# Reordering the masks, the lower product and the spread in a chunked delta rule

## The reference

```python
g = jnp.cumsum(chunks(g), axis=-1)
decay = jnp.exp(jnp.where(tri_incl, g[..., :, None] - g[..., None, :], -jnp.inf))
k_beta = k * beta[..., None]
lower = jnp.where(tri_strict, jnp.einsum('nbhid,nbhjd->nbhij', k_beta, k) * decay, 0.0)
rhs = jnp.concatenate([v * beta[..., None], k_beta * jnp.exp(g)[..., None]], -1)
sol = lax.linalg.triangular_solve(lower + jnp.eye(CHUNK, dtype=f32), rhs,
                                  left_side=True, lower=True, unit_diagonal=True)
u, w = sol[..., :DV], sol[..., DV:]
attn = jnp.where(tri_incl, jnp.einsum('nbhid,nbhjd->nbhij', q, k) * decay, 0.0)
...
def step(state, xs):
    v_new = u_c - jnp.einsum('bhck,bhkv->bhcv', w_c, state)
    o = jnp.einsum('bhck,bhkv->bhcv', q_c, state) + jnp.einsum('bhij,bhjv->bhiv', attn_c, v_new)
    state = state * jnp.exp(gl)[..., None, None] + jnp.einsum('bhck,bhcv->bhkv', k_c, v_new)
```

## Time and profile before

| | us |
|---|---|
| Median of 3 runs | 3335.11 |
| Lowest and highest run | 3326.7, 3336.2 |
| Profiled execution, its own time | 3328.85 |
| Span of the profiled execution, first to last instruction | 3327.4 |
| TensorE busy in the span | 3072.8 |
| VectorE, ScalarE, GpSimd busy in the span | 1593.7, 1075.9, 1077.9 |

### The profile page before, as it was taken

One profiled execution on the slowest core, in us unless ns is written; L12 is line 12 of the kernel. 1 busy time (PEld: TensorE's weight loads), 2 busy tenths in 40 slices (PEclk: granted clock), 3 DMA queues, 4 the chain that ended last, 5 costly groups with the idle time before them and its releaser, 6 DMA issues. The chain is left out here.

```text
span 3327.4 us, 44247 instructions
## 1 busy us (share of the span) xinstructions
PE 3072.8 (92%) x15074; PEld 2540.9 (76%) x15074; DVE 1593.7 (48%) x2713; ACT 1075.9 (32%) x2399; POOL 1077.9 (32%) x1209
## 2 busy tenths in 40 slices
PE   6999997959998899989979999899998999999898
PEld 5888885648786788878768888788887788887686
DVE  3554004535664555556585455865555433233433
ACT  2211004334544555542243333433333211111321
POOL 2222241066665766410073333543331000000122
PEclk9999998979998999999989999999999999999999
DMA  3212115422324211125723222232223333233443
GB/s 136 88 75 77 76 57 168 156 76 67 82 72 107 59 52 53 67 77 178 239 69 122 91 76 83 69 117 93 77 79 110 132 98 101 91 95 117 154 123 99
DMA packets 284414, 329.18 MB, mean 99 GB/s; under 512 B 33281, under 2 KB 224641, under 8 KB 279937
## 3 DMA queue, kind: packets, MB, share of 16 engines
q1 hardware_dynamic: 238632, 265.84, 25.1%
q0 software_dynamic: 12384, 45.09, 3.8%
q10 hardware_dynamic: 33280, 16.78, 1.8%
HBM read 210.73 MB, written 116.92 MB: 98 GB/s over the span
## 5 line engine op out<-in xcount | busy, mean ns | idle before, releaser
L2074 PE MATMUL ff_bank<-ff_x_hi,ff_w_lo 128*128 128x512 f32 x1240 | 487.6, 393 | 31.7 <-DVE ff_w_lo L2254 22.2
L2075 PE MATMUL ff_bank<-ff_x_lo,ff_w_hi 128*128 128x512 f32 x1240 | 486.5, 392 | 0.0
L2076 PE MATMUL ff_bank<-ff_x_hi,ff_w_hi 128*128 128x512 f32 x1240 | 486.3, 392 | 0.0
L2057 POOL TENSOR_TENSOR ff_w_sum<-ff_w_raw 128x512 f32<-128x512 f32 x210 | 301.2, 1444 | 492.4 <-DVE ff_w_lo L2254 434.0
L296 PE MATMUL in_h_ps<-in_x_hi,in_w_lo 128*128 128x512 f32 x704 | 277.5, 394 | 25.7 <-POOL in_w_lo L252 25.7
L2074 PEld LDWEIGHTS ff_bank<-ff_x_hi,ff_w_lo 128*128 128x128 f32 x1240 | 235.4, 190 | 84.0 <-DVE ff_w_lo L2254 25.0
L2464 PE MATMUL fd_acc<-fd_w_hi,fd_a_lo 128*128 128x512 f32 x704 | 279.2, 397 | 11.5 <-DVE fd_a_lo L2448 11.5
L2466 PE MATMUL fd_acc<-fd_w_hi,fd_a_hi 128*128 128x512 f32 x704 | 280.4, 398 | 0.0
L2465 PE MATMUL fd_acc<-fd_w_lo,fd_a_hi 128*128 128x512 f32 x704 | 278.4, 395 | 0.0
L297 PE MATMUL in_h_ps<-in_x_lo,in_w_hi 128*128 128x512 f32 x704 | 276.8, 393 | 0.0
L298 PE MATMUL in_h_ps<-in_x_hi,in_w_hi 128*128 128x512 f32 x704 | 276.4, 393 | 0.0
(11 more groups left out here) (381 smaller groups left out, 6558.5 us busy)
## 6 DMA issues: line engine op xcount, KB each, us to landing
ff_w_raw<-w_gate_up SPq DMA_DIRECT2D x44, 1024.0 KB, 5.2
scratch_hT<-in_out SPq DMA_DIRECT2D x22, 1024.0 KB, 3.9
fd_a_raw<-scratch_hid SPq DMA_DIRECT2D x176, 128.0 KB, 2.1
dr_qkv<-scratch_hT SPq DMA_DIRECT2D x16, 768.0 KB, 5.1
in_w_raw<-w_in POOLq DMA_DIRECT2D x22, 512.0 KB, 3.9
scratch_hid<-ff_first SPq DMA_DIRECT2D x44, 256.0 KB, 2.3
scratch_hid<-ff_second SPq DMA_DIRECT2D x44, 256.0 KB, 2.3
fd_w_raw<-w_down SPq DMA_DIRECT2D x22, 512.0 KB, 5.0
```

The source lines that it names most:

```text
L2057: pool.tensor_tensor(w_sum[:, SUM_SLOT[m]], w_raw[:, b, one], w_raw[:, b, two], op).then_inc(w_sum_done, 1)
L2074: pe.matmul(acc, w_lo[:, wm, ws], x_hi[:, xm, k], start=first_mm, stop=False, skip_group_check=skip)
L2075: pe.matmul(acc, w_hi[:, wm, ws], x_lo[:, xm, k], start=False, stop=False, skip_group_check=skip)
L2076: return pe.matmul(acc, w_hi[:, wm, ws], x_hi[:, xm, k], start=False, stop=last_mm, skip_group_check=skip)
```

## The change

GpSimd makes the mask below the diagonal first, then the other, and both of them before the decayed q. The factor of L's rows is no longer multiplied in by GpSimd; VectorE takes it as the scalar of an instruction that multiplies twice, one for each head. The k by k product gets a semaphore of its own, on which L waits. VectorE spreads the inverses ahead of attention's product.

```diff
-        gram_done = s.sem("gram_done")
+        gram_k_done, gram_done = s.sem("gram_k_done"), s.sem("gram_done")
...
-                    sp.wait_ge(masked, 3 * TILES)
+                    sp.wait_ge(masked, 2 * TILES)
...
             def masks(m):
                 pool.wait_ge(dec_done, m + 1)
+                reached(pool, L_done, m)
+                pool.tensor_tensor(dec[:, 0], dif[:, m % 2], each(below[:]), ALU.mult).then_inc(masked, 1)
                 reached(pool, attn_done, m)
                 pool.tensor_tensor(dec[:, 1], dif[:, m % 2], each(upto[:]), ALU.mult).then_inc(masked, 1)
-                reached(pool, L_done, m)
-                pool.tensor_tensor(dec[:, 0], dif[:, m % 2], each(below[:]), ALU.mult).then_inc(masked, 1)
-                pool.wait_ge(masked, 3 * m + 2)
-                pool.wait_ge(made_done, 3 * (m + 1))
-                pool.tensor_tensor(dec[:, 0], dec[:, 0], heads(made[:, m % 2, 2]), ALU.mult).then_inc(masked, 1)
...
                 if m is not None:
+                    masks(m)
                     decayed(m)
-                    masks(m)
...
                 for h in range(HEADS):
-                    pe.matmul(b0[:, h], qkv[:, m % 3, HEADS + h], qkv[:, m % 3, HEADS + h], start=True, stop=True)
+                    last = pe.matmul(b0[:, h], qkv[:, m % 3, HEADS + h], qkv[:, m % 3, HEADS + h], start=True, stop=True)
+                last.then_inc(gram_k_done, 1)
...
-                reached(act, masked, 3 * (m - 1))
+                reached(act, masked, 2 * (m - 1))
...
-                reached(dve, masked, 3 * (m - 1))
...
             def p_lower(m):
-                dve.wait_ge(gram_done, m + 1)
-                dve.wait_ge(masked, 3 * m + 3)
+                dve.wait_ge(gram_k_done, m + 1)
+                dve.wait_ge(masked, 2 * m + 1)
...
-                dve.tensor_tensor(L[:, m % 3], b0[:], dec[:, 0], ALU.mult).then_inc(L_done, 1)
+                for h in range(HEADS):
+                    op = dve.scalar_tensor_tensor(L[:, m % 3, h], b0[:, h], made[:, m % 2, 2, h:h + 1], dec[:, 0, h],
+                                                  ALU.mult, ALU.mult)
+                op.then_inc(L_done, 1)
 
             def p_attention(m):
                 dve.wait_ge(gram_done, m + 1)
+                dve.wait_ge(masked, 2 * m + 2)
...
                 if first:
                     p_lower(m)
-                    p_attention(m)
                 if base:
                     spread(e)
+                if first:
+                    p_attention(m)
```

## The result

The changed kernel takes 3301.11 us in the median of four executions (3300.12 to 3303.30). Four of the kernel before, the three that the prediction had and one more, have a median of 3330.90. The ratio is 0.9922, with a 95% interval of 0.9901 to 0.9942: 26 us less, between 19 and 33 (the two medians alone are 30 apart). The forecast was 3316, in 3306 to 3330. Two sizes are involved: the base of 3335.1 was the median of three executions and stood 4 to 9 us above what more executions gave (3326.2 to 3330.9 in five sets of 4 to 35), and the gain itself was under-sized. The profiled executions leave the base out: 3328.85 before and 3301.84 after (span 3300.4) are 27.0 apart, where 18.7 were forecast. So 8.3 us are to be explained.

What follows compares the result with a forecast made beforehand. The substitution loop was taken to bound most delta-rule rounds, just above TensorE's own order. Terms of 1.9, 1.7, 13.9 and 1.2 made 18.7 us off 3335.1, giving 3316 us, in 3306 to 3330.

Steps and rivals of the forecast that it cites:

- Masks: L, behind GpSimd's `below` alone, starts 1.35 after the substitution instead of 4.86, 3.5 us less; decays ready with 0.4 to spare.
- L on VectorE: Four instructions that multiply twice take 1.12 us against 0.69 for L, adding 0.43 to the substitution loop.
- Own signal: L's gate from TensorE comes 2.7 us earlier, serving the five rounds that waited for k by q.
- substitution loop: Delta-rule round from one store of the inverses through L, its store, blocks' load and substitution to the next: 20.75 us.
- TensorE's order: TensorE's own work in a delta-rule round, from L1151 to the end of L1180: 19.68 us.
- The queue, the 19.9 loop: L's early store lands 1.05 behind the inverses on the DMA queue, so the changed substitution loop takes 19.9 us, not 17.65.
- Attention's product and the norm: Attention's product, now behind the spread on VectorE, delays the norm and so L1096: counted as 0.1 us a round.
- Term (3): The 13 delta-rule rounds give back 17.8 us of waits for U less 3.9 for loop and attention's product: 13.9 us.
- Term (4): At the last spread, L of tile 15 ends 2.2 us earlier, 1.0 of it counted in term (3): 1.2 us gained.
- Queue keeps the loop: Rival: L's store takes its whole 2.0 behind the inverses, loop 20.85; 7.5 us gained, 3328; chance 0.26.
- No queueing: Rival: L's store lands in 2.0 wherever issued, loop 17.65, TensorE binds; 27 us gained, 3308; chance 0.15.
- Slower: Rival: inverses land late and hold up VectorE's order; 10 us lost if landing takes 9.4, 3345; chance 0.07.

Runs made afterwards that it cites:

- masks_only: The changed kernel with L waiting for k by q and attention's product ahead of the spread, as before the change: 3325.05 us, ratio 0.9975 to the kernel before.
- undo_signal: The changed kernel without k by k's own signal, so L waits for k by q again: 3324.41 us, ratio 0.9993 to the kernel before.
- load_last: The changed kernel with a later tile's q, k, v load issued behind L's store and its blocks' load: 3295.21 us, ratio 0.9907 to the kernel before.
- spread6: The changed kernel with its spread written six times, to make TensorE wait for U: 3364.19 us, ratio 1.0100 to the kernel before.
- load_last_tail: load_last with five loads for the next stage issued behind the load of the last inverses: 3298.58 us, ratio 0.9905 to the kernel before.
- the filled kernels: The kernel before with extra identity products ahead of TensorE's wait for U: eight took 3328.11 us, four took 3333.19 us.
- no_masks: The kernel before with k by k's own signal and the spread's new place, GpSimd's masks and factor unchanged: 3324.69 us, ratio 0.9987.
- spread_only: The kernel before with only the spread moved ahead of attention's product: 3326.38 us, ratio 1.0000.
- before_filled4: The kernel before with four extra identity products ahead of TensorE's wait for U: 3333.19 us, ratio 1.0012.
- spread6_filled: spread6 with eight identity products on TensorE ahead of its wait for U: 3354.03 us, ratio 1.0069 to the kernel before.

## Why the prediction fell short, point by point

**Masks.** As forecast: `below` is GpSimd's first operation behind a substitution, L never waits for it in the 13 rounds, and L starts 3.08 after the inverses' store in place of 4.86. The cover of 0.4 us for the decays was not there: the substitution ends 12.8 us after L1149 and the decays 13.4, where I had 13.4 and 13.0, and `below` waits for ScalarE in 10 rounds. It costs nothing, since k by k ends later still, as the forecast had said.

**L on VectorE.** 1.13 us against 0.69, as priced (+0.43), and the undisturbed 21.08 of `masks_only` against 20.65 fits it.

**Own signal.** Forecast as serving the five rounds that k by q held up. It serves all of them: without it the change is worth 2 us (`undo_signal`), and with it alone some 5. I had the substitution loop (20.75) and TensorE's order (19.68) and took the k by q waits for the slow clock's doing. By `masks_only` the chain through k by q and VectorE, 20.65 a round, ran beside them the whole time. The sum was not hurt, since the change opens both; a forecast of the parts would have been.

**The queue, the 19.9 loop.** Its rule was tested in the first rounds alone. There L's store is issued while the big load and the inverses' load are under way:

```profile
702.09 0.38 SPq L977 DMA_DIRECT2D dr_u_blk<-scratch_blocks_U  x1
703.07 0.44 SPq L980 DMA_DIRECT2D scratch_blocks_L<-dr_L  x1
706.85 1.38 SPq L987 DMA_DIRECT2D dr_blk<-scratch_blocks_L  x4
```

The store takes 3.8 us and the blocks' load goes out 3.78 behind its issue, some 0.5 behind the landing of the inverses. I had taken 1.05 behind it, between 0.8 and 2.0, so the sign was right and the price too high, the lower bound included. That a store is told of only behind the earlier transfers is the order which the Trainium skill states ("DMA: Bandwidth & Descriptors", section Queues, rings and completion order). The trace agrees: 3.8 us instead of 2.0, without the full 2.0 that I had added for the strictest case. In the steady rounds it doesn't arise: k by k, not the mask, lets L go, its store is issued 4.24 after the inverses' and lands in 2.0. The loop of 19.9 doesn't bind there.

**Attention's product and the norm.** I counted 0.1 a round for it. The waits show 0.3 to 0.5 us at L1093 in 6 of the rounds (such a round takes 19.9 to 20.2 instead of 19.47), and `load_last` shows their cause: the inverses land 4.2 after their issue, the spread is late, and the norm behind it. Over the 12 rounds that is 0.31 a round. So my deduction of 3.9 us and the measured 3.7 agree in size by luck: what takes them is the inverses' load, not L's store.

**Term (3), the step that failed.** It reads "if nothing but TensorE bound them they would give back all 17.8", less 3.9. Per round that is 21.57 - 13.9 / 13 = 20.50; measured are 19.78, 0.72 less, 8.6 us over 12 rounds. What was wrong with it is that it removed the waits and kept all the rest of the round as it stood. Without the waits for U (16.85 us in these 12 rounds) TensorE took 242.0 us before and takes 237.3 after, against its own 12 x 19.47 = 233.6. Nearly all of the 8.6 is the difference between those 242.0 and 233.6; the 3.7 above them is what I had deducted anyway. Two things had been inside the 242.0. One is the slow clock. I wrote "slow clock included" in what would show the forecast, and so held it to be a property of the stage. It stood in three stretches, 13.6 us in sum, each right behind a wait of 1.77 to 1.96 us at L1151; one of them:

```profile
819.55 0.44 PE L1151 MATMUL dr_b<-dr_ident,dr_U 128*128 128x128 f32 x2 [1.96 <-DVE dr_U L1449]
824.18 1.97 PE L1096 MATMUL dr_b<-dr_ident,dr_qkv 128*128 128x128 f32 x8
```

The eight transposes in the second row take 1.09 us at full clock, a round later. What the stretches cost can be read in this trace: without the wait that ends it, each of the nine rounds at full clock takes 19.68 or 19.69, and the three with a stretch take 21.15, 22.57 (23.53 - 0.96) and 21.16. That is 1.47 + 2.89 + 1.48 = 5.8 us, 0.43 for each us at 1.2 GHz. That these stretches went because the waits went is not shown by an experiment in this kernel: `spread6` shows that such waits can cost the clock, and neither of the two traces of the change has a stretch at 1.2 GHz between 740 and 988 us. The other thing is TensorE's round itself: I read 19.68 off one round, and every full-clock round of this trace has it, but 19.47 is what a round needs that holds no wait for U, 0.21 x 12 = 2.5 us. The three add up: 233.6 + 5.8 + 2.5 = 241.9. So term (3) took TensorE's time between the waits for fixed, and 8.4 us of it were not.

**Term (4).** -0.1 in place of 1.2. L of the last tile ends 1.2 earlier against the reader of its round, as forecast, but the queue takes it back. L's store takes 2.50 where it took 2.04 (983.97 to 986.47 against 1011.99 to 1014.03; no run says why), and the load of the last inverses goes out later:

```profile
999.68 0.33 SPq L968 DMA_DIRECT2D scratch_blocks_U<-dr_inv  x1
1002.99 0.37 SPq L977 DMA_DIRECT2D dr_u_blk<-scratch_blocks_U  x1
```

```profile
1005.64 0.44 PE L1149 MATMUL dr_b<-dr_ident,dr_U 128*128 128x128 f32 x2 [2.00 <-DVE dr_U L1450]
```

From the store to the load are 3.31 us; the kernel before has 2.41 at this place and both have 1.5 in an ordinary round. In `load_last_tail`, where attention's first five loads are issued behind it, it is 1.50: it is those loads on the queue that delay the store. TensorE waits 2.00 for this U, against 1.75 before.

**Rivals.** "Queue keeps the loop" is out: no wait for U is left in 13 rounds. "No queueing" named 27 us and 3308, and 27.0 is what the profiled executions show, but not for its reason: the store of L does queue where it is early, and the waits of 17.8 were given back together with 4.7 of TensorE's own time (8.4 less the 3.7 of the late norm). It had a chance of 0.15, and its number came right by luck. "Slower" did not occur; the inverses' landing is 4.2 in the median and 4.9 at most.

**Still open.** What brings a stretch at 1.2 GHz is not settled by the length of a wait: in the kernel before 1.77 to 1.96 us did and 2.43 (at 906.73) did not, the filled kernels and `no_masks` have a stretch behind 1.45, and `spread_only` none behind 2.94. Nor is it settled what the 5.8 us were worth in time while both chains stood. `before_filled4` takes 4.1 us less over the 12 rounds with a whole clock, and `spread_only`, which has one too, 3.1 less (pace 21.31); these are single executions of kernels with another order, and neither is faster as a whole. So some 3 to 4 us is an estimate, and the rest of the 5.8 came only with the two chains.

## What to carry to other kernels

Write down every chain that closes on itself in a round, the short waits that look harmless included, and compare their lengths: here 20.65, 20.75 and 19.47. Where two are within 0.1 us, freeing one is worth little and freeing both is worth their whole distance to the third, so a part that measured little alone may carry most of the gain: the signal gave 5 us, hardly clear of nothing, and its removal takes all but 2. Find the bound's own time for a round in the round with no idle and full clock, not in a typical one, and ask of each wait of 1.5 to 2 us on TensorE whether a stretch at 1.2 GHz stands behind it. On a DMA queue put a small load that someone waits for ahead of a big one that is needed a round later: moving one issue took the pace from 19.78 to 19.47, and the times suggest some 5 us more (the intervals overlap).

## What was not expected of the hardware

- 2.34 us of idle ahead of each U in an otherwise busy round brought ten stretches at 1.2 GHz in twelve rounds, 3.4 to 10.2 us each, and cost 1.5 us a round; eight products of the identity in the idle time took them away (`spread6`, `spread6_filled`). A stretch was seen behind 1.45 us of idle, and none behind another 2.94. Each us at 1.2 GHz cost this mix of small matmuls 0.40 us in `masks_only` and 0.43 in the kernel before, not 0.50.
- The inverses' load takes 4.2 us in the median behind the 768 KB load on its queue, and 1.8 to 2.0 in `load_last`, where that load goes out later; a store of L behind both took 3.8 instead of 2.0.
- Four `scalar_tensor_tensor` of 128 x 128, one for each head and with one operand in PSUM, take 1.13 us together where one product of the same 512 columns takes 0.69.
